# Recurrence stage of a hybrid encoder: order of a load, of three memsets, the engine of the samples' decayed keys, and the signal of the diagonals

## What is computed

```python
def gated_delta(q, k, v, g, beta, s0, chunk):      # chunk 64 for the prompt, 16 (= t) for the samples
    ...
    gc = jnp.cumsum(g, axis=-1)
    decay = jnp.exp(jnp.where(causal, gc[..., :, None] - gc[..., None, :], NEG))
    kb = k * beta
    lower = jnp.where(strict, jnp.einsum("...id,...jd->...ij", kb, k) * decay, 0.0)
    rhs = jnp.concatenate([v * beta, kb * jnp.exp(gc)[..., None]], -1)
    sol = lax.linalg.triangular_solve(lower + jnp.eye(chunk, dtype=F32), rhs,
                                      left_side=True, lower=True, unit_diagonal=True)
    u, w = sol[..., :dv], sol[..., dv:]
    intra = jnp.where(causal, jnp.einsum("...id,...jd->...ij", q, k) * decay, 0.0)

    def step(s, inp):
        q_i, k_i, u_i, w_i, gc_i, a_i = inp
        v_new = u_i - jnp.einsum("bhck,bhkv->bhcv", w_i, s)
        o = (jnp.einsum("bhck,bhkv->bhcv", q_i * jnp.exp(gc_i)[..., None], s)
             + jnp.einsum("bhcs,bhsv->bhcv", a_i, v_new))
        g_last = gc_i[..., -1:]
        s = (s * jnp.exp(g_last)[..., None]
             + jnp.einsum("bhck,bhcv->bhkv", k_i * jnp.exp(g_last - gc_i)[..., None], v_new))
        return s, o
```

## Time and profile before

| what | value |
|---|---|
| timed runs, median of 3 | 3611.88 us (3608.4 to 3614.02) |
| the profiled execution, its own time | 3604.7 us |
| its span, first to last instruction | 3603.2 us |
| TensorE matmul busy | 3350.1 us, 93% |
| TensorE weight loads busy | 3003.7 us, 83% |
| VectorE, ScalarE, GpSimd busy | 2097.7, 1473.9, 443.6 us |
| mean granted TensorE clock | 0.964 of full |

### The profile page before, as it was taken

The page is one execution under the profiler, slowest core; times in us unless marked ns, Lnnn a source line. Parts: engine busy times, 40 slices in busy tenths (PEclk is TensorE's granted clock), DMA queues, the critical chain, the costliest instruction groups (busy, mean ns, idle before and its releaser), DMA issues. The chain is left out here.

```text
span 3603.2 us, 67992 instructions
## 1 busy us (share of the span) xinstructions
PE 3350.1 (93%) x27025; PEld 3003.7 (83%) x27025; DVE 2097.7 (58%) x3523; ACT 1473.9 (41%) x2819; POOL 443.6 (12%) x671
## 2 busy tenths in 40 slices
PE   7999999976899996999697799999999999999997
PEld 7899999944788884666586798998999999899995
DVE  2655556654345444666487465665565565575695
ACT  2434444443244443666343343343343343343353
POOL 0000000021456552000133000000000000000000
PEclk8999999987899997999898899999999999999999
DMA  7677766741111115332475644454454454454464
GB/s 225 179 221 225 212 183 185 198 134 39 37 41 41 36 29 179 124 122 85 154 221 186 190 138 152 126 176 149 126 171 151 129 175 147 128 171 141 141 193 131
DMA packets 706406, 521.44 MB, mean 145 GB/s; under 512 B 64648, under 2 KB 650615, under 8 KB 706043
## 3 DMA queue, kind: packets, MB, share of 16 engines
q1 hardware_dynamic: 658312, 427.16, 40.3%
q0 software_dynamic: 26576, 70.12, 5.6%
q10 hardware_dynamic: 21216, 19.93, 1.8%
HBM read 432.11 MB, written 86.05 MB: 144 GB/s over the span
## 5 line engine op out<-in xcount | busy, mean ns | idle before, releaser
L1219 PE MATMUL ps_gate_up<-h2T_group_high,w_gate_up_high 128*128 128x384 f32 (+1 forms) x2112 | 689.5, 326 | 23.7 <-DVE w_gate_up_low L1315 17.4
L1220 PE MATMUL ps_gate_up<-h2T_group_low,w_gate_up_high 128*128 128x384 f32 (+1 forms) x2112 | 688.5, 326 | 0.0
L1221 PE MATMUL ps_gate_up<-h2T_group_high,w_gate_up_low 128*128 128x384 f32 (+1 forms) x2112 | 688.4, 326 | 0.0
L1219 PEld LDWEIGHTS ps_gate_up<-h2T_group_high,w_gate_up_high 128*128 128x128 f32 x2112 | 398.7, 189 | 26.4 <-issue 26.4
L1220 PEld LDWEIGHTS ps_gate_up<-h2T_group_low,w_gate_up_high 128*128 128x128 f32 x2112 | 398.8, 189 | 0.0
L1221 PEld LDWEIGHTS ps_gate_up<-h2T_group_high,w_gate_up_low 128*128 128x128 f32 x2112 | 398.7, 189 | 0.0
L1315 DVE TENSOR_TENSOR w_gate_up_low<-w_gate_up,w_gate_up_high 128x1024 fp32r<-128x1024 f32 x264 | 322.3, 1222 | 63.1 <-ACT w_gate_up_high L1253 51.6
L1321 DVE TENSOR_TENSOR w_down_low<-w_down_ring,w_down_high 128x512 fp32r<-128x512 f32 x264 | 182.4, 693 | 290.9 <-ACT w_down_high L1259 290.7
L1253 ACT ACTIVATE w_gate_up_high<-w_gate_up 128x1024 fp32r<-128x1024 f32 x264 | 279.1, 1057 | 162.0 <-PE ps_gate_up L1221 136.8
L1259 ACT ACTIVATE w_down_high<-w_down_ring 128x512 fp32r<-128x512 f32 x264 | 166.0, 631 | 331.7 <-PE ps_down L1231 166.0
L433 PE MATMUL ps_feature<-hT_high,w_in_high 128*128 128x384 f32 (+1 forms) x816 | 271.6, 333 | 9.8 <-DVE hT_low L607 8.4
(11 more groups left out here) (445 smaller groups left out, 6647.9 us busy)
## 6 DMA issues: line engine op xcount, KB each, us to landing
w_gate_up<-in_w_gate SPq DMA_DIRECT2D x132, 512.0 KB, 3.7
w_gate_up<-in_w_up SPq DMA_DIRECT2D x132, 512.0 KB, 3.8
w_down_ring<-in_w_down SPq DMA_DIRECT2D x264, 256.0 KB, 2.6
w_in_ring<-in_w_in SPq DMA_DIRECT2D x84, 512.0 KB, 4.2
w_ada_ring<-in_w_ada SPq DMA_DIRECT2D x48, 512.0 KB, 5.2
s_ck_rows<-in_cache_c_k SPq DMA_DIRECT2D x32, 512.0 KB, 6.8
s_cv_rows<-in_cache_c_v SPq DMA_DIRECT2D x32, 512.0 KB, 5.0
d_convT<-scratch_convT SPq DMA_DIRECT2D x17, 576.0 KB, 4.3
```

The source lines that it names most:

```text
L1219: pe.matmul(out, w_high, h_high, start=(k == 0), stop=False)
L1220: pe.matmul(out, w_high, h_low, start=False, stop=False)
L1221: last = pe.matmul(out, w_low, h_high, start=False, stop=(k == DC - 1))
```

## The change

Four edits, all in `stage_delta`:

- SyncE issues `load(2)` right after `load(1)` has landed, ahead of the wait for `blank_ready` and of the samples' states. `load(3)` stays behind the states.
- GpSimd's `log_diag` gives its signal once for each half of the heads instead of once for the tile, and TensorE's `exponents(n, half)` waits for its own half.
- The instructions of `s_k_decay` leave GpSimd. ScalarE does them as eight activations with the column of `in_seq` as scale, after `norm_logs(1)` and ahead of its loop.
- VectorE's three memsets go from behind `sums_copied(1)` to between `scale_kv(0)` and `matrices(0, 0)`.

```diff
@@ SyncE
             load(0)
             sp.wait_ge(loaded[0], 32)
             load(1)
+            sp.wait_ge(loaded[1], 32)
+            load(2)
             sp.wait_ge(s["blank_ready"], 1)
             for hh in range(2):
                 ...
-            load(2)
             load(3)
@@ GpSimd, log_diag
-                last.then_inc(s["diag_ready"], 1)
+                    last.then_inc(s["diag_ready"], 1)
@@ GpSimd, sample_operands
                 pool.sem_inc(s["s_qT_ready"], 1)
-                for b in range(DEC_B):
-                    last = pool.tensor_tensor(s_k_decay[:, b], k_decay[:, late(0)], in_seq[:, 1, b:b + 1].to_broadcast([P, W]),
-                                              ALU.mult)
-                last.then_inc(s["s_k_decay_ready"], 1)
@@ TensorE
             def exponents(n, half):
-                pe.wait_ge(s["diag_ready"], n + 1)
+                pe.wait_ge(s["diag_ready"], 2 * n + half + 1)
@@ ScalarE
+            def sample_decays():
+                act.wait_ge(s["kv_ready"], 1)
+                for b in range(DEC_B):
+                    last = act.activation(s_k_decay[:, b], k_decay[:, late(0)], ACT.Identity, scale=in_seq[:, 1, b:b + 1])
+                last.then_inc(s["s_k_decay_ready"], 1)
             ...
             softplus(1)
             norm_logs(1)
+            sample_decays()
             for k in range(TILES + 2):
@@ VectorE
             scale_kv(0)
+            for t in (s_state, s_wT, s_qT):
+                last = dve.memset(t[:], 0.0)
+            last.then_inc(s["blank_ready"], 1)
             matrices(0, 0)
             matrices(0, 1)
             decays(1)
             sums_copied(1)
-            for t in (s_state, s_wT, s_qT):
-                last = dve.memset(t[:], 0.0)
-            last.then_inc(s["blank_ready"], 1)
```

## The result

The changed kernel takes 3596.77 us (median of 6 runs, 3595.14 to 3597.73) against 3610.62 us of the kernel before, measured beside it (6 runs, 3608.4 to 3616.54): 13.85 us less, ratio 0.9958, 95% interval 0.9946 to 0.9971. The profiled executions have spans of 3603.2 and 3593.6 us, 9.6 us apart. The recurrence (the stage), from SyncE's first issue in it to the first of the next stage, took 1387.77 - 858.82 = 528.95 us before and takes 1379.00 - 859.00 = 520.00: 9.0 us less.

The account below looks back on a forecast made before the run. At the recurrence's start TensorE waits 7.7 us behind memsets, states and tile 2's load; later TensorE bounds itself. -7.6 - 1.4 + 0.2 - 1.5 = -10.3 us off the 3611.88 us median gives 3601.6 us, range 3598.6 to 3603.7.

Parts of the forecast that it names:

- I take the difference off the median: 3601.6 us: Whole kernel: the 10.3 us gain taken off 3611.88 us, the median of three timed runs, gives 3601.6 us.
- The sum of the parts: Start of the recurrence: -7.6 load, -1.4 memsets, +0.2 ScalarE's keys, -1.5 clock; -10.3 us, bounds -8.2 and -13.3.
- rival B: VectorE's moved memsets and GpSimd exclude each other: 3.9 us more, 3605.5 to 3607 us, no measurable change; 13%.
- C: Gain taken back, above all by sample_faded: matrices(1, 0) not before 917.5, 6.7 us left, 3605.2 us; 10%.
- D: TensorE's products of the samples left at half clock: 7.7 us slower, 3619.6 us; 5%.
- So matrices start at 915 ... and `s_faded` takes what is beyond: VectorE, tile 1: s_faded runs from 911.2 to 914.9, so matrices start at 915 against 924.20; 9 us hold.
- The term of the clock: TensorE, start of recurrence: gaps gone, half-clock work gets shorter; 1.5 us off, nothing at worst.
- TensorE bounds every later tile: Recurrence from 1040 to 1375 us: TensorE busy 320.85 of 335 us at full clock, its own bound.
- The load was priced at -7.6: SyncE issues load(2) first: exponents of tile 1 could start at 911.2 instead of 918.84 us, -7.6 us.
- the memsets at -1.4: VectorE's memsets moved: +3.2 us before matrices(0, 0), -4.6 us at the copy of X, net -1.4 us.
- that chain: Start of recurrence: memsets, states' issue, tile 2's load, soften(2), log_diag(1), exponents of tile 1, where TensorE waits 7.7 us.
- The keys' move: Decayed keys from GpSimd to ScalarE: avoids a possible collision with s_faded, worth 0 to 3.7 us, counted 0.

Follow-up runs that it names:

- memsets apart: Changed kernel with its three memsets set apart: after scale_kv(0), after matrices(0, 0), after sums_copied(1); states' load waits for the first alone; 3590.98 us, ratio 0.9956.
- the keys also moved: Changed kernel with the memsets set apart and ScalarE's decayed keys ahead of norm_logs(1) instead of behind it; 3588.26 us, ratio 0.9946.

## Why the prediction was right or wrong

**The step that failed: "I take the difference off the median: 3601.6 us".** The sum of the parts, -10.3 us, was put on 3611.88 us, the median of three runs, and the range 3598.6 to 3603.7 got its width from the parts alone: the base was given none, though those three runs lay 5.6 us apart. The changed kernel measured 3596.77 and, again, 3597.10 us. All 66 timed runs of the kernel before on record have a median of 3608.7 us, 3.2 us below the base; the same sum with the same bounds would then reach from 3595.4 to 3600.5 us. On the profiled execution, where base and result are of one kind, the same sum gave 3594.4 us, and 3595.14 and 3594.06 were measured. So the failed term is the base, and the sum was near. Inside the sum several terms were off too, and that they cancelled is in part luck, as follows.

**The moments came as forecast.** Matrices at 884.86 (forecast 884.6), next product at 899.33 (899.4), diagonals at 901.88 (901.7), keys of 4.14 us (4.2), exponents of tile 1 at 907.92 (908 to 910). The memsets did not hold GpSimd back: its diagonals beside them took 0.97 to 0.98 us for two, as in the earlier trace rows. So the prediction's rival B fell. So did C (the matrices of tile 1 start at 912.24, not at 917.5 or later) and D (the samples' 48 products take 5.62 us, as before).

**"So matrices start at 915 ... and `s_faded` takes what is beyond" was mis-sized.** They start at 912.24: `s_faded` began at 908.97, not 911.2, and took 3.35 us, while the one of 3.67 us in the earlier trace rows had GpSimd's diagonals beside it. The forecast let the matrices start no earlier than 915, whatever TensorE gained before them. With the upper clock from 900.4 on, the gain at tile 1's first mask was 12.5 us, where 9.2 and 1.5 for the clock had been forecast.

**The term of the clock was then partly given back.** The clock fell at 914, and the three sets from 924.17 took 1.52, 1.52 and 1.33 us, where the same sets of the kernel before took 1.36, 0.88 and 0.88, the last two at the upper level from 937.7. At the samples' products the gain was 11.4 us (929.64 against 941.01). The prediction also read two rises of the clock where the trace of the kernel before has three between 890 and 940 us. The first came at 896.8, just after TensorE had run out of work, and was over at 900.2, before it had any again: it went by in the 4.60 us wait for the copy of X. The others came at 907.0 and 937.7. In the changed kernel TensorE is at work when the clock rises at 900.4.

**"TensorE bounds every later tile" missed a wait.** Counted from the stage's start, the gain is 11.55 us at the samples' products and 8.95 us at the stage's end: 2.6 us were lost in between. TensorE's wait for the copy of X grew by just as much, from 6.3 to 8.9 us, and the time of the later 14 tiles from 370.1 to 372.7 us. A tile takes mostly 26.15 or 26.9 us in these traces. VectorE in a tile of each sort, and TensorE's product that waits for the copy of X behind it, first the kernel before, then the changed one:

```profile
1029.17 0.16 DVE L3101 TENSOR_SCALAR d_norm_logs<-d_norm_logs 128x6 f32<-128x6 f32 x1
1029.40 0.81 DVE L3104 TENSOR_TENSOR d_factor_logs<-d_sums,d_norm_logs 128x6 f32<-128x6 f32 x1
1030.13 0.15 DVE L3105 TENSOR_TENSOR d_factor_logs<-d_sums,d_norm_logs 128x6 f32<-128x6 f32 x1
1030.21 0.97 DVE L3106 TENSOR_TENSOR d_minus_gc<-d_norm_logs,d_sums 128x6 f32<-128x6 f32 x1
1031.25 0.88 DVE L3108 TENSOR_TENSOR d_factor_logs<-d_factor_logs 128x6 f32<-128x6 f32 x1
```

```profile
1033.72 1.06 PE L2634 MATMUL ps_d_LX<-d_inverse,d_minus_L 64*64 64x64 f32 x24 [0.33 <-DVE d_inverse L3131]
```

```profile
1017.79 1.05 DVE L3105 TENSOR_SCALAR d_norm_logs<-d_norm_logs 128x6 f32<-128x6 f32 x1
1018.91 0.88 DVE L3108 TENSOR_TENSOR d_factor_logs<-d_sums,d_norm_logs 128x6 f32<-128x6 f32 x1
1019.72 1.03 DVE L3109 TENSOR_TENSOR d_factor_logs<-d_sums,d_norm_logs 128x6 f32<-128x6 f32 x1
1020.68 1.03 DVE L3110 TENSOR_TENSOR d_minus_gc<-d_norm_logs,d_sums 128x6 f32<-128x6 f32 x1
```

```profile
1023.10 1.18 PE L2631 MATMUL ps_d_LX<-d_inverse,d_minus_L 64*64 64x64 f32 x24 [1.09 <-DVE d_inverse L3135]
```

Instructions of 0.16 us last 0.8 to 1.05 where GpSimd's 1.0 us masks run beside them; three are caught in the first tile, four in the second, and TensorE's wait for the copy of X behind them is 0.33 us in the first and 1.09 in the second. How many tiles are hit differs between executions: the 14 tiles took 370.1 and 370.8 us in the two traces of the kernel before, 372.7 and 373.1 in those of the changed one, and 370.1 to 374.0 in the kernels with one part alone or left out, with no order by edit. Copying X ahead of `row_low` brought TensorE's wait from 8.9 to 4.8 us and took 5.2 us off the stage. That such hits make the spread of the runs is not shown: with this wait halved the runs lay 8.5 us apart.

**The division among the parts was wrong, though the sum was near.** The load was priced at -7.6 and the memsets at -1.4. Alone, the load does bring 7.6 us at the exponents; but both edits free one chain, and the prices can't be given to the parts one by one. With the load alone 6.3 us go at tile 1's inverse, with the memsets alone 11.5. Taken out of the changed kernel, the load costs 0 and the memsets 1.0 us. What the memsets add depends on the rest: with the keys on GpSimd and one signal for a tile, the kernels of load alone and of memsets alone lie 5.2 us apart. I had followed the memsets to TensorE but not past SyncE, though that chain stood in my own first paragraph. The keys' move, counted at nothing between 0 and 3.7, brings 1.0 us at tile 1's inverse, and over the whole stage no gain by it is seen.

**The total.** The forecast was 10.3 us. The stage shows 9.0 and 9.5 (against its two traces before), the spans 9.6 to 11, the second timing 10.1. The first timing gave 13.85, its interval reaching from 10.5 to 19.5 (of 0.9971 and 0.9946). The excess lies in the six runs of the kernel before, whose median was 1.8 to 4.5 us above those of its later runs, while the changed kernel's two medians are 0.3 us apart. Why those six runs took longer stays open; no trace of one of them is on record.

## What to carry to other kernels

When a step is moved, follow every signal it gives, through the DMA queue too: two edits that free the same chain don't add, and testing each alone and each left out shows it. Look for the gaps on the engine where a moved step will stand, and cut the step to fit them: three memsets apart, in gaps that the trace already showed, took 4.7 us more off the stage than the three together. A wait of a third of a microsecond to one microsecond in every tile is worth reading even where an engine is 96% busy: cutting it took 5.2 us off the stage. And a forecast of a time stands on its base: give the base a width of its own, from the spread of the runs, or forecast the difference.

## What was not expected of the hardware

Three plain memsets of 128x3072 start 3.21 us apart though each row reads 2.62: before each the profile shows 0.59 us of idle time for which it names no wait, so a memset is best counted at 3.21 us. VectorE's small instructions on SBUF (128x6) last until the mask that GpSimd has running beside them is over, one mask for each: 0.16 us becomes 0.81 to 1.05. The Trainium skill (SBUF — State Buffer, Who interferes with whom) names as contending with GpSimd the VectorE instruction with two SBUF inputs and the two-port modes, which it says `tensor_scalar` can enter; the row of 1.05 us at L3105, a `tensor_scalar` with one input, agrees with that. The prediction gave the half of that rule on instructions with one input without the two-port modes; for the memsets it made no difference. An earlier start of TensorE's work did not always bring an earlier rise of its clock: with the first matrices 5.1 us earlier (memsets apart) the rise came 0.4 us later into the stage, and with the keys also moved it came 3.1 us earlier. Why the first of these orders gained nothing in clock stays open.
